# Second prompt tile's memory attention moved behind the first routing, one routing head at a time, new buffer places, shorter side loads

## The reference, cut to what matters

```
z = x @ w_in                                   # then HGRN2 heads and sparse attention
x = LN(alpha*x + concat(heads) @ w_out)
x = LN(alpha*x + softmax((x@w_mem_q) . mem_k / 16) . mem_v @ w_mem_o)      # 256 memory rows, 4 heads of 256
qh = x @ peer_w_q                              # 1024 -> 8 heads x 2 halves x 128
s = qh . sub_keys                              # 128 keys per half
s1,i1 = top16(half 0); s2,i2 = top16(half 1); best 16 of the 256 sums -> 16 experts per head
h = gelu(x . peer_u[e]);  y = sum(softmax(score) * h * peer_v[e])
x = LN(alpha*x + y)
```

## Time and profile before

| | us |
|---|---|
| Median of 3 runs | 1339.42 (1337.71 to 1348.48) |
| Profiled execution, its own time | 1332.73 |
| Span of its records | 1330.9 |
| PE busy | 850.7 (64%) |
| DVE busy | 720.6 (54%) |
| POOL busy | 651.9 (49%) |
| ACT busy | 224.5 (17%) |
| DMA of POOL's queue | 318.82 MB, 61.3% of 16 engines |
| DMA of SP's queue | 110.46 MB, 24.0% of 16 engines |

### The profile page before, as it was taken

How to read it: one execution, slowest core, us unless ns; L and a number is a source line. 1 busy time by engine, 2 the same in 40 slices (tenths; PEclk the granted TensorE clock), 3 DMA queues, 4 the chain that set the end, 5 groups by cost and what they waited for, 6 DMA issues and landing times.

```text
span 1330.9 us, 12875 instructions
## 1 busy us (share of the span) xinstructions
PE 850.7 (64%) x4531; PEld 437.6 (33%) x4531; DVE 720.6 (54%) x1806; ACT 224.5 (17%) x431; POOL 651.9 (49%) x631
## 2 busy tenths in 40 slices
PE   7999899998878786849535444353652444333354
PEld 5666554455434554537213120021220111000000
DVE  1233773122686773687676782486365543855431
ACT  2211441122122332201211210121120011000000
POOL 3000100000077677766777774467573554777762
PEclk9999899999999798877667776677686666666667
DMA  6874233532399999999999999999999999999995
GB/s 222 208 218 128 72 127 116 191 135 95 109 348 408 388 410 395 397 396 362 407 388 409 407 409 340 411 411 412 412 410 400 409 394 396 399 367 410 410 371 232
DMA packets 146319, 430.10 MB, mean 323 GB/s; under 512 B 26064, under 2 KB 33680, under 8 KB 143056
## 3 DMA queue, kind: packets, MB, share of 16 engines
q0 software_dynamic: 87168, 318.82, 61.3%
q1 hardware_dynamic: 59088, 110.46, 24.0%
HBM read 422.31 MB, written 6.52 MB: 322 GB/s over the span
## 4 chain that ended last, share of the span: by engine, by line
PE 34%; DMA 30%; POOL 21%; issue 8%; DVE 5%; ACT 2%; SPq 0%; POOLq 0%; DVEq 0%; ACTq 0%
DMA u<-in_peer_u,Ei 19%; PE banks L1864 18%; POOL v L824 11%; POOL u L824 9%; DMA v<-in_peer_v,ETi 8%; PE banks L1804 4%; PE banks L1871 2%; DMA wbuf<-in_w_in 2%; DVE u L1296 1%; PE banks L2269 1%; PE banks L2028 1%; PE banks L2181 1%; DMA wbuf<-in_peer_w_q 1%; PE banks L2220 1%; POOL slv L824 1%
## 5 line engine op out<-in xcount | busy, mean ns | idle before, releaser
L1296 DVE CUSTOM_DVE_ANT_0 u<-u,xt 128x1024 f32<-128x1024 f32 x288 | 351.4, 1224 | 318.4 <-DMA u<-in_peer_u,Ei 316.5
L824 POOL DMA_INDIRECT u<-in_peer_u,Ei x288 | 291.9, 1014 | 425.0 <-DVE E L1275 221.0
L1804 PE MATMUL banks<-v,wz 128*32 128x512 f32 x1104 | 216.9, 914 | 321.1 <-DMA v<-in_peer_v,ETi 290.9
L824 POOL DMA_INDIRECT v<-in_peer_v,ETi x276 | 303.2, 1099 | 93.0 <-issue 79.9
L1804 PEld LDWEIGHTS banks<-v,wz 128*32 128x32 f32 x1104 | 43.0, 144 | 435.2 <-issue 414.4
L839 POOL TENSOR_TENSOR z<-z,par 128x512 f32<-128x512 f32 x2 | 2.6, 1294 | 122.5 <-ACT zs L974 122.5
L1864 PE MATMUL banks<-wbuf,x2T 128*128 128x512 f32 x128 | 58.2, 609 | 5.9 <-issue 2.6
L2220 PE MATMUL banks<-subT,w1s 128*128 128x252 f32 x256 | 57.6, 383 | 0.0
L1864 PE MATMUL banks<-wbuf,memT 128*128 128x512 f32 x128 | 55.9, 593 | 0.0
L2220 PEld LDWEIGHTS banks<-subT,w1s 128*128 128x128 f32 x256 | 48.5, 193 | 14.9 <-issue 7.5
L1864 PE MATMUL banks<-wbuf,xT 128*128 128x512 f32 (+1 forms) x128 | 49.7, 546 | 0.6 <-DMA wbuf<-in_w_in 0.6
(11 more groups left out here) (450 smaller groups left out, 1252.1 us busy)
## 6 DMA issues: line engine op xcount, KB each, us to landing
wbuf<-in_w_in SPq DMA_DIRECT2D x4, 2048.0 KB, 16.0
wbuf<-in_peer_w_q SPq DMA_DIRECT2D x4, 2048.0 KB, 9.9
mck<-in_cache_mem_k SPq DMA_DIRECT2D x8, 1024.0 KB, 15.2
mcv<-in_cache_mem_v SPq DMA_DIRECT2D x8, 1024.0 KB, 13.0
ws<-in_peer_w_q SPq DMA_DIRECT2D x4, 2048.0 KB, 18.9
u<-in_peer_u,Ei POOLq DMA_INDIRECT x288, 9.4
v<-in_peer_v,ETi POOLq DMA_INDIRECT x276, 10.1
wbuf<-in_w_mem_k SPq DMA_DIRECT2D x2, 2048.0 KB, 9.3
```

The source lines that it names most:

```text
L824: return nc.gpsimd.indirect_dma_start(out=dst, out_offset=None, in_=table, in_offset=bass.IndirectOffsetOnAxis(ap=index, axis=0)).then_inc ...
L1296: v.tensor_tensor_reduce(out=uslot[n % USLOTS][:, :], in0=uslot[n % USLOTS][:, :], in1=xt[:, g // 4, :], scale=1.0, scalar=0.0, op0=ALU.mu ...
L1804: ins = mm(psum[32 * j:32 * j + 32, c, :], wz[:, o % 2, i, j, :], vbuf(m + j)[:, GW * c:GW * c + GW], start=first, stop=last)
```

## The change

Four things are done. (1) Tile 1's memory attention (`mq`, `mqT`, `ms`, `mpT`, `mo`, `mw`) moves behind the first routing. Only half of `mq` stays ahead, where PE waits for a norm. The scores of group 0 are computed and routed one head at a time (`pqa`, `pqTa`, `psa`), and ACT makes the copies of the second head. (2) Buffers are placed anew, with five weight buffers. The first two u slots do not overlap the weights that are still in use, so POOL starts step 0 when head 0 is routed (`e_half`), step 2 when `mq` 1 is filled and step 16 when head 1 is routed. (3) The step numbers of the side jobs are dealt anew: `mw` of tile 1 at step 13, quads up to 43, the compressed keys from 46 in blocks of 11 steps, all later ones 8 steps later. The early v rows start at step 16. The last routing runs at k = 17 to 24 with six instructions a step. (4) The norm rows of the sample are loaded for 32 partitions and not 128. `w1s` (twice) and `skeys` are loaded in long contiguous rows in place of rows of 512 B, and PE's transposes or ACT's copies put the order right.

```diff
-V_EARLY = 12
+V_EARLY = 16
 def prompt_jobs():
...
-    jobs += [("mqT", 0, k) for k in range(2)] + [("mq", 1, c) for c in range(2)]
-    jobs += [("ms", 0, k) for k in range(2)] + [("mqT", 1, k) for k in range(2)] + [("mv", 0, 0)]
-    jobs += [("ms", 1, k) for k in range(2)] + [("mv", 0, 1)] + [("mv", 1, t) for t in range(2)]
+    jobs += [("mqT", 0, k) for k in range(2)] + [("mv", 0, 0)]
+    jobs += [("ms", 0, k) for k in range(2)] + [("mv", 0, 1)] + [("mv", 1, t) for t in range(2)]
     jobs += [("mpT", 0, k) for k in range(2)] + [("mo", 0, k) for k in range(2)] + [("mw", 0, c) for c in range(2)]
-    jobs += [("mpT", 1, k) for k in range(2)] + [("skeyT", q) for q in range(4)] + [("mo", 1, 0)]
+    jobs += [("skeyT", q) for q in range(4)] + [("mq", 1, 0)]
     jobs += [("x2T", 0, c) for c in range(2)]
-    return jobs + quad_jobs(0, 0) + [("mo", 1, 1)]
+    return jobs + [(name, r) for r in range(2) for name in ("pqa", "pqTa", "psa")]
...
 SIDE = [
-    ([("mw", 1, c) for c in range(2)], 0, 0),
-    (quad_jobs(0, 1), 1, 1), (quad_jobs(0, 2), 4, 5),
-    ([("x2T", 1, c) for c in range(2)], 7, 7),
-    (quad_jobs(1, 0), 9, 10), (quad_jobs(1, 1), 13, 14), (quad_jobs(1, 2), 18, 19),
-    (quad_jobs(0, 3), 23, 24), (quad_jobs(1, 3), 28, 29),
-    *cmp_jobs(34),
+    ([("mq", 1, 1), ("mqT", 1, 0), ("mqT", 1, 1), ("ms", 1, 0), ("ms", 1, 1)], 0, 0),
+    (quad_jobs(0, 1), 1, 1),
+    ([("mpT", 1, k) for k in range(2)] + [("mo", 1, k) for k in range(2)], 2, 2),
+    ([("mw", 1, c) for c in range(2)], 13, 13),
+    (quad_jobs(0, 2), 15, 15), ([("x2T", 1, c) for c in range(2)], 18, 18),
+    (quad_jobs(1, 0), 22, 23), (quad_jobs(1, 1), 28, 29), (quad_jobs(1, 2), 34, 34),
+    (quad_jobs(0, 3), 38, 38), (quad_jobs(1, 3), 42, 43),
+    *cmp_jobs(46),
...
-    ([("pqp", c) for c in range(2, 4)], 226, 226), ([("pqs", c) for c in range(2, 4)], 227, 227), ([("pqTs",), ("pss",)], 229, 230),
+    ([("pqp", c) for c in range(2, 4)], 234, 234), ([("pqs", c) for c in range(2, 4)], 235, 235), ([("pqTs",), ("pss",)], 237, 238),
...
+W_GROUPS = [...
+            ("w_mem_q", 0, ("mq", 1, 0), 2), ("w_mem_q", GW, ("mq", 1, 1), 3), ("w_mem_v", 0, ("mv", 0, 1), 1), ("w_mem_v", GW, ("mv", 1, 1), 0),
+            ("w_mem_o", 0, ("mw", 1, 0), 4), ("w_mem_o", GW, ("mw", 1, 1), 1),
+            ("peer_w_q", 0, ("pq", 1, 0), 0), ("peer_w_q", GW, ("pq", 1, 1), 2), ("peer_w_q", 2 * GW, ("pq", 1, 2), 1), ("peer_w_q", 3 * GW, ("pq", 1, 3), 0)]
+W_OFFSETS = (32, 16, 0, 62, 110.25)
...
-    uslot = [at(f"u{k}", 62 + 4 * k, [P, D]) for k in range(USLOTS)]
+    uslot = [at(f"u{k}", 62 + 4 * ((k + 4) % USLOTS), [P, D]) for k in range(USLOTS)]
...
+    def copy_first(eng, r):
+        two = slice(2 * r, 2 * r + 2)
+        for name, dst in (("pqa", pqst[:, two, :]), ("pqTa", pqT[0][:, two, :]), ("psa", sc[:, 0, two, :])):
+            key = (name, r)
+            if (eng is nc.scalar) == (r == 1 or name == "psa"):
+                filled(eng, key)
+                src = split(bank(key)[:, 0:256], P)
+                release(eng, nc.scalar.copy(dst, src) if eng is nc.scalar else nc.vector.tensor_copy(dst, src), key)
...
@@ sync
-        sp.dma_start(w1s[:, :, :], w1_dram[0]).then_inc(s_cws, 16)
+        sp.dma_start(w1s[:, :, :].rearrange("p (f c) h -> p f c h", f=2), w1_wide[0]).then_inc(s_cws, 16)
...
-        norm_rows(lnps, 1, s_lnps)
+        norm_rows(lnps, 1, s_lnps, NS)
...
-                sp.dma_start(skeys[:, :, :], A["peer_sub_keys"][0].rearrange("h c k d -> k (h c) d")).then_inc(s_skeys, 16)
+                sp.dma_start(skeys[:, :, :], A["peer_sub_keys"][0].rearrange("h c k d -> (h c k) d").rearrange("(p j) d -> p j d", j=16)).then_inc(s_skeys, 16)
...
@@ gpsimd
-        cmp_at = [28, 30, 39] + [...]
+        cmp_at = [40, 42, 50] + [...]
...
-                if k == 0:
+                if n == 0:
+                    pool.wait_ge(e_half, 1)
+                    filled(pool, ("mw", 0, 1))
+                elif n == 2:
+                    filled(pool, ("mq", 1, 1))
+                elif k == 0 or n == PICK // 2:
                     pool.wait_ge(e_ready, 2 * g + 2)
-                if n == 0:
-                    filled(pool, ("skeyT", 3))
-                    filled(pool, ("mw", 0, 1))
-                    filled(pool, ("mv", 1, 1))
...
@@ vector
-        def experts(g):
+        def experts(g, first=0, count=2):
+            heads, hh, kk = range(first, first + count), slice(first, first + count), slice(16 * first, 16 * (first + count))
...
+            v.tensor_copy(Ei[:, g % 2, kk], Ef[:, kk]).then_inc(e_ready if first + count == 2 else e_half, 1)
...
-                    late = 8 if g == NGRP - 2 else 0
+                    start, last, each = (17, 24, 6) if g == NGRP - 2 else (4, 20, 3)
...
-        copy_quad(dve, 0, 0, 0)
-        filled(dve, ("mpT", 1, 1))
-        for _ in experts(0):
-            pass
-        gates(0)
+        for r in range(2):
+            copy_first(dve, r)
+            for _ in experts(0, r, 1):
+                pass
+        mem_max(1)
...
+        stream.upto(1)
+        mem_weighted(1)
         residual("mw", 1)
         norm(1, small[:, 170:190], s_lnv, s_lnr, 4, None, None, s_ln)
-        stream.upto(36)
+        stream.upto(44)
         affine(1)
@@ tensor
-        all_evacuated([("skeyT", q) for q in range(4)])
-        quad(0, 0, 0)
-        mem_values(1, [1])
-
+        all_evacuated([("skeyT", q) for q in range(4)] + [("x2T", 0, c) for c in range(2)])
+        wt = landed(WG["peer_w_q", 0])
+        for r in range(2):
+            o = begin(("pqa", r))
+            for k in range(KC):
+                ins = mm(o[:, 0:256], x2T[0][:, k, :], wt[:, k, 256 * r:256 * r + 256], start=(k == 0), stop=(k == KC - 1))
+            done(ins, ("pqa", r))
...
+        mem_queries(1, [1])
+        turn_queries(1)
+        mem_scores(1)
+        quad(0, 1, 1)
+        pace(pe, ("mpT", 1, 0))
+        turn_mem(1)
+        mem_values(1)
         pace(pe, ("mw", 1, 0))
         all_evacuated([("mo", 1, k) for k in range(2)])
         by_tile("mw", "w_mem_o", 1)
-        quad(0, 1, 1)
         quad(0, 2, 2)
...
-                    ins = tr(o[:, P * m:P * m + P], rows[:, P * n:P * n + P], ident)
+                    g, c = q // 2, 4 * (q % 2) + m
+                    ins = tr(o[:, P * m:P * m + P], rows[:, D * g:D * g + D].rearrange("p (k c) -> p c k", c=8)[:, c, :], ident)
```

More of the change, by code:

```diff
@@ L171, in cmp_jobs @@
         jobs += [(pages[1][0:2], s + 2, s + 2), (pages[1][2:4], s + 3, s + 3)]
-        jobs += [([("hid", kv, half, g)], s + 7 + 4 * g, s + 7 + 4 * g) for g in range(2)]
-    return jobs + [([("cmp",) + HALVES[-1]], first + 48, first + 48)]
+        jobs += [([("hid", kv, half, g)], s + 6 + 4 * g, s + 6 + 4 * g) for g in range(2)]
+    return jobs + [([("cmp",) + HALVES[-1]], first + 44, first + 44)]
 def key_jobs(u, b):
@@ new lines @@
+    (quad_jobs(0, 1), 1, 1),
[5 more added lines that the diff above has]
+    *cmp_jobs(46),
+    ([("att", 2), ("kE", 2)], 90, 91),
+    ([("oin", 2), ("ost", 2)], 93, 94),
+    ([("US", b) for b in range(N_SAMPLE)], 95, 99),
@@ L247, in w_value @@
 def w_value(n):
-    return 16 * sum(W_DMAS[i] for i in range(n % 3, n + 1, 3))
+    return 16 * sum(W_DMAS[i] for i in range(n + 1) if W_BUF[i] == W_BUF[n])
 def s_value(n):
@@ L1253, in experts @@
                 yield
-            yield from best16([(cv[:, r], cj[:, r], cand[:, r]) for r in range(2)])
-            V(v.tensor_tensor(texp[:, :, :], cv[:, :, :], cv[:, :, 0:1].to_broadcast([P, 2, 16]), ALU.subtract), s_tmx)
+            yield from best16([(cv[:, r], cj[:, r], cand[:, r]) for r in heads])
+            V(v.tensor_tensor(texp[:, hh, :], cv[:, hh, :], cv[:, hh, 0:1].to_broadcast([P, count, 16]), ALU.subtract),
+              s_tmx if first + count == 2 else None)
             yield
-            flat = cj[:, :, :].rearrange("p h k -> p (h k)")
@@ L1261, in experts @@
             yield
             for c in range(2):
[L1263 removed]
+                V(v.tensor_tensor(eqm[:, kk, :], bc(jaf[:, c, kk], 2, 16), bc(C("iota16"), 1, n), ALU.is_equal))
                 yield
[L1265 removed]
+                for r in heads:
                     rows = slice(16 * r, 16 * r + 16)
[L1267 removed]
+                    V(v.tensor_tensor(eqm[:, rows], eqm[:, rows], bc(tif[:, r, c], 1, 16), ALU.mult), wait=(r == heads[-1]))
@@ L1319, in peer @@
                 if g < NGRP - 1:
-                    late = 8 if g == NGRP - 2 else 0
-                    if k == 4 + late:
+                    start, last, each = (17, 24, 6) if g == NGRP - 2 else (4, 20, 3)
+                    if k == start:
                         route = experts(g + 1)
-                    if 4 + late <= k < 20:
-                        for _ in range(3 + late // 8):
+                    if start <= k < last:
+                        for _ in range(each):
                             next(route, None)
-                    if k == 20:
+                    if k == last:
```

(2 more changed lines are left out.)

250 lines of the change are left out of this document (128 added, 122 removed).

## The result

| | before | after |
|---|---|---|
| Median | 1339.04 us (1337.71 to 1348.48, 4 runs) | 1324.16 us (1322.02 to 1328.25, 4 runs) |
| Ratio, 95% interval | | 0.9893 [0.9854, 0.9931] |
| Profiled execution, span | 1332.73, 1330.9 | 1328.25, 1326.5 |

The change saves 14.9 us by the medians; forecast were 14.3. The two profiled executions lie only 4.5 us apart: the one of before is faster than all four timed beside it, the one of after the slowest of its four. So the traces tell where time is won and lost, and the medians how much. The sum came out right, but three of its six terms did not (the ramp, the quads, the last routing), and a fourth, the long rows, stays open.

A forecast was written before the change was run, and what follows sets the result against it. The saturated DMA stream sets the end: its start, its work and its gaps. Terms 10.6 + 1.9 - 4 - 1.5 + 3.8 + 3.5 = 14.3 us, off the median 1339.4, give 1325 us; range 1310 to 1341.

The forecast's parts named there:

- the ramp: Window 380 to 400 lost 4.9 us before; the new kernel meets this for steps 13 to 18 only, losing 3: +1.9.
- the quads: Query quads dealt anew: a late weight group makes DVE wait 10 us near 421, slots and page gather cover 10.2: -4.
- the last routing: Scores still ready 4.5 us ahead, but eight steps hold the routing where nine did: -1.5 us, bounds 0 and -5.
- the long rows: Three loads in rows of 512 B lower the DMA rate; long rows save 3.5 us, bounds 0 and 5.
- The timeline: First phase to the quads: first gather near 332.3, 29.5 us earlier; 17 gathers out by 372; quad (1,2) ends near 432.
- the signs of being wrong: First v gather before 360, no stall near 420 to 435, or PE's transposes several times longer.
- Head start: Gathers and weight loads by 372: lead 5.0 MB, 12.2 us, less 1.6 to refill the queue: +10.6; bounds 4 and 16.
- Norm rows: Four row blocks loaded for 32 partitions: 1.57 MB less, 3.8 us saved.
- (a): The wait is covered: PE runs ahead, the quads' stall stays inside the slots, the ramp is clean; gain 24, 1315; chance 0.22.
- (b): Quads starve the stream: full 10 us lost, early v batches wait too; gain 5, 1334; chance 0.19 together with (d).
- (d): Head start is spent: chain to 372 slips, routing at the end starves; gain 1, 1338; chance 0.19 together with (b).
- (c): Page transposes at a 32 B stride slow PE: at five times 1358, at five and a half 1368; chance 0.09.

The follow-up runs named there:

- Experiment 5: The changed kernel, but POOL waits for the routing of both heads of group 0 before its first gather; 1327.06 us, ratio 0.9909.
- experiment 6: The changed kernel with quad (1,2) of the queries at step 35 instead of 34, behind the gate transposition; 1324.29 us, ratio 0.9878.
- experiment 7: The changed kernel with the last three quads later, at steps 38, 42 and 45, and the compressed branch one step later; 1329.15 us, ratio 0.9898.
- Experiment 9: The changed kernel with two quads of tile 1 ahead of quad (0,2), whose weights land late; 1322.05 us, ratio 0.9858.
- experiment 4: The changed kernel run once more, unaltered; 1326.89 us, ratio 0.991.
- Experiment 8: The changed kernel with the short tile's second-half queries three to four steps later and the last routing at steps 19 to 25; 1324.73 us, ratio 0.9881.
- experiment 1: The kernel before, with only the sample's norm rows loaded for 32 partitions; 1332.86 us, ratio 0.997.
- experiment 3: The changed kernel with the old side loads: norm rows on 128 partitions, `w1s` and `skeys` in rows of 512 B; 1332.56 us, ratio 0.9952.
- experiment 2: The kernel before, with only `w1s` and `skeys` loaded in long rows, with the strided transposes and copies needed; 1338.14 us, ratio 0.9997.

## Why the prediction was right, and where it was not

**The timeline** held within 2.2 us: `mpT` of tile 0 at 284.9 (282.7 forecast), the product of half width at 316.6 (315.7), the first gather at 333.85 (332.3), 17 u gathers before the first v gather at 372.71 (372), the weight group at 383.9 (385), quad (1,2) ended near 430.6 (432). The hole ahead of 372 was there too (157 and 126 GB/s in 345 to 350 and 350 to 355), and none of the signs of being wrong showed. Two readings in the text are off and change nothing in the sum: the filler ahead of `x2T` is priced at about 3 us where its own numbers give 4.8 (311.9 less 303.1 and 4.0), and page transposes are said to take 0.27 us as before, where the earlier trace rows has 0.315.

**Head start, +10.6.** Measured +10.2 and +13.9 in two executions. Counting at 372 and not at the first gather was right: 28 us at the first gather are 10 to 14 in bytes. In all eleven profiles of the change and its variants the lead at 380 is 10 to 15 us. Experiment 5 sharpens it: of those 28 us, 9 are worth nothing that can be seen.

**The ramp, +1.9.** Measured +4.9: 408 GB/s in 380 to 400, in both executions. The step that failed is the assumption that steps 13 to 18 meet the old ramp of the earlier trace rows: nothing was lost where 3 us had been put down. It is not that DVE was free. The second routing went on to 391.3, and DVE was busy for 17.1 us of the window instead of 19.6:

```profile
391.30 0.18 DVE L1304 CAST Ei<-Ef 128x32 int32<-128x32 f32 x1
```

What differs by 380 is the queue: the v gathers had begun at 372.71 and not at 382.01, and a weight group of 2.1 MB, landed at 383.9, lay beside them. Which of the two kept the DMA engines full was not tested.

**The quads, -4.** Measured -6.9. The cause was named rightly (a weight group that lands late, then a quad ahead of the gates), but the cover of 10.2 us was not there. DVE waited 5.5 us, not 10, and yet more was lost. In 417 to 426 POOL already waited for DVE before four of its u gathers, so the slots held no reserve. The v rows waited behind the same quads (experiment 6), and experiment 7 shows that a later place only moves the hole. Experiment 9 takes away what stands in front of everything else, PE's 11.95 us without work, and with it DVE's wait and 1.5 to 3.7 us of the loss; the rest has no cause that a run shows.

**The last routing, -1.5.** Measured -5.7 and -7.5 in 1120 to 1300, against the one execution of before. I looked only at the slack of the scores. Their copy ended 2.0 us ahead of DVE's first instruction on them (4.5 forecast), and that was no wait:

```profile
1138.32 0.60 ACT L504 ACTIVATE scs<-banks 128x512 f32<-128x512 f32 x1 [2.16 <-PE banks L2546]
```

```profile
1140.92 0.87 DVE L1261 MAX8 tv<-scs 128x8 f32<-128x128 f32 x4
```

What I left out is the weight loads for those queries, 9.64 and 7.24 us of PE's time in which v batches stood behind it. Before had such waits too (8.73 and 6.18 us), so it is not their length but what they now hold up: POOL stood 9.86 us for PE in after and 6.03 in experiment 4, where it had stood 2.05 at most. Experiment 8 takes them away. How much of the loss is theirs and how much the denser routing's is open, since it moved both. How much belongs to the change at all is open too: experiment 1 moved 386 GB/s in 1120 to 1300, 4 less than before, and the low rates from 1180 on with it.

**Norm rows, +3.8.** 4.0 alone by the ratio, 7.4 by the medians. The bytes were counted rightly, but that 32 partitions load at the full rate was assumed: the dip to 316 GB/s takes back 0.9 us at the second pair of rows (the first loads right behind `w_out`, where it cannot be told apart). **Long rows, +3.5.** 0.4 alone, 1.6 by difference, 2.6 in windows; the times do not exclude 3.5. Too large, if anything, is the first dip of the earlier trace rows, put at 1.5 us, where experiment 3 shows 0.8 for that load. The Trainium skill, "DMA: Bandwidth & Descriptors", Specifications, has 512 B as enough for line rate. The times agree with it within their interval; the windows of experiment 3 do not (376, 388 and 373 GB/s against 410, 408 and 406 at full DMA share), so the measurement gives 5 to 8% there.

**The sum.** Against the forecast's 14.3 the ledger has -0.4 for the head start, +3.0 for the ramp, -2.9 for the quads, -4.2 for the last routing, and -2.4 in 460 to 1120 where I had +3.5 for long rows: 3.9 in all. The medians say 14.9. The trace of before lies 6.3 us under the median of its four runs and that of after 4.1 over its own, which is nearly the whole difference. No trace of before itself near its median was read, so where those executions lose their time is open. Experiment 1's trace lies at its own median and has the low rates from 1180 on, which may be such a place. By its own base, 1332.7 less 14.3, the forecast would have been 1318.4, and the profiled execution of after took 1328.25. It was the step to the median's basis that brought the number home: right for the medians, though not by a mechanism that a trace shows. That the two numbers lie 0.6 us apart is luck: the terms are off by up to 6 us each in the ledger, the interval of the ratio reaches from 9 to 20 us, and experiment 4 has 13.4. That something near the sum was gained is more than luck: experiments 3 and 4 measure its two halves, 6.4 us where 7.0 were forecast for the moved work and 5.6 where 7.3 were for the side loads.

**The rivals.** (a) had its clean ramp but neither of the other two conditions. (b) is what happened in 400 to 460, at 7 us instead of 10. (d)'s late starving came, without the slipped chain. (c) falls:

```profile
L2254 PE MATMUL banks<-cst,subg 128*128 128x128 f32 x128 | 18.3, 298 | 14.4 <-ACT subg L1101 14.4
L2254 PEld LDWEIGHTS banks<-cst,subg 128*128 128x128 f32 x128 | 16.2, 197 | 19.1 <-issue 19.1
```

The transposes at a stride of 32 B take 298 ns against 315 in the earlier trace rows, and 316 in experiment 2, where nothing else of the schedule was changed. The Trainium skill, "SBUF — State Buffer", Door 1, lets an access pay that leaves its 16-byte line; on PE's products nothing of that is seen here.

## What to carry over

Count a head start in bytes at the first point where the queue stands anyway, not at its first transfer: the 9 us of the first head were worth nothing. When a side job stalls a stream, ask what made the engine late before moving the job: two moves shifted the hole, and filling the idle time ahead of it took at least a part of it away. Compare a trace with its own median before trusting a small difference between two: here the two lay 10 us apart by that alone. For every step that is dealt anew, list the loads that it waits for, not only the results that wait for it.
